# Reordering the attention steps of a hybrid encoder: first scores, two projection tiles and the transposes of V

## The reference

```
for l in range(2):
    h = rms_norm(x, attn_norm_g[l]);  parts = split(h @ w_in[l])
    ya = banded_attention(rope(qa), rope(ka), va, 128, sink)      # 8 query heads, 2 kv heads
    for window, dilation in ((128, 1), (512, 4), (2048, 16)):     # 4 heads each
        o, lse = dilated_attention(rope(qg), rope(kg), vg, window, dilation)
    yb = sum(softmax(lse) * o)                                     # over the three groups
    x = x + (sigmoid(gA) * (ya @ w_branch_a) + sigmoid(gB) * (yb @ w_branch_b)) @ w_out
    x = x + hier_moe(rms_norm(x, ffn_norm_g[l]))                   # 32 experts, two per token
return rms_norm(x, final_norm_g)
```

## Time and profile before

| | us |
|---|---|
| median of 3 runs (lowest, highest) | 1330.33 (1329.66, 1333.43) |
| span of the profiled execution | 1327.3 |
| PE busy | 1199.9 (90%) |
| DVE busy | 548.4 (41%) |
| ACT busy | 408.8 (31%) |
| POOL busy | 242.5 (18%) |
| idle of PE before its weight matmuls of the experts, waiting for their DMA | 38.4 |

### The profile page before, as it was taken

The page is one execution under the profiler, slowest core; times in us unless marked ns, Lnnn a source line. Parts: engine busy times, 40 slices in busy tenths (PEclk is TensorE's granted clock), DMA queues, the critical chain, the costliest instruction groups (busy, mean ns, idle before and its releaser), DMA issues.

```text
span 1327.3 us, 17358 instructions
## 1 busy us (share of the span) xinstructions
PE 1199.9 (90%) x6332; PEld 787.9 (59%) x6332; DVE 548.4 (41%) x1376; ACT 408.8 (31%) x822; POOL 242.5 (18%) x179
## 2 busy tenths in 40 slices
PE   7999998999988998889589999899999999988981
PEld 5777777888875443333177777778887844433320
DVE  4557664323344322222355676553333442322115
ACT  5344456333242111001244444563323411110002
POOL 0324510222201111111012353002221011111100
PEclk9999999999998999999899999999999999999996
DMA  5333311653746999999833333126437479999995
GB/s 199 114 98 101 96 57 34 206 189 100 255 171 213 404 425 422 425 422 412 320 96 103 96 96 96 33 87 218 156 110 286 166 273 410 423 423 424 420 412 232
DMA packets 69438, 305.97 MB, mean 231 GB/s; under 512 B 11968, under 2 KB 12224, under 8 KB 59120
## 3 DMA queue, kind: packets, MB, share of 16 engines
q1 hardware_dynamic: 58624, 282.45, 56.8%
q0 software_dynamic: 10592, 21.71, 4.4%
q10 hardware_dynamic: 144, 0.77, 0.2%
HBM read 289.68 MB, written 23.07 MB: 236 GB/s over the span
## 4 chain that ended last, share of the span: by engine, by line
PE 67%; DMA 16%; SPq 5%; DVE 5%; ACT 4%; issue 2%; DVEq 1%; POOLq 0%; ACTq 0%
PE bank L541 14%; PE bank L543 13%; PE bank L542 13%; DMA gu<-in_gu_w 12%; PE bank L840 10%; PE bank L856 4%; SPq L400 4%; DMA raw<-in_stream 2%; PE bank L650 2%; PE bank L679 2%; SPq L405 2%; PE bank L614 1%; PE bank L835 1%; PE bank L783 1%; DMA yld<-y_rows 1%
## 5 line engine op out<-in xcount | busy, mean ns | idle before, releaser
L840 PE MATMUL bank<-gu,xgt 128*64 128x512 f32 x1024 | 240.2, 619 | 40.1 <-DMA gu<-in_gu_w 38.4
L541 PE MATMUL bank<-h_hi,w_hi 128*128 128x512 f32 x640 | 253.1, 395 | 4.5 <-DVE h_lo L1280 3.5
L543 PE MATMUL bank<-h_hi,w_lo 128*128 128x512 f32 x640 | 249.4, 390 | 0.0
L542 PE MATMUL bank<-h_lo,w_hi 128*128 128x512 f32 x640 | 249.1, 389 | 0.0
L1235 DVE TENSOR_TENSOR w_lo<-raw,w_hi 128x1024 fp32r<-128x1024 f32 x102 | 131.2, 1287 | 176.9 <-ACT w_hi L968 176.9
L840 PEld LDWEIGHTS bank<-gu,xgt 128*64 128x64 f32 x1024 | 75.2, 142 | 201.1 <-issue 151.9
L541 PEld LDWEIGHTS bank<-h_hi,w_hi 128*128 128x128 f32 x640 | 120.2, 188 | 29.5 <-issue 3.4
L543 PEld LDWEIGHTS bank<-h_hi,w_lo 128*128 128x128 f32 x640 | 120.1, 188 | 25.4
L542 PEld LDWEIGHTS bank<-h_lo,w_hi 128*128 128x128 f32 x640 | 120.3, 188 | 23.8
L968 ACT ACTIVATE w_hi<-raw 128x1024 fp32r<-128x1024 f32 x102 | 107.4, 1053 | 59.7 <-PE bank L543 56.2
L856 PE MATMUL bank<-dn,zt 128*64 128x512 f32 x512 | 117.0, 599 | 6.3 <-ACT zt L1196 2.8
(11 more groups left out here) (186 smaller groups left out, 1596.3 us busy)
## 6 DMA issues: line engine op xcount, KB each, us to landing
gu<-in_gu_w SPq DMA_DIRECT2D x18, 4096.0 KB, 33.0
raw<-in_stream SPq DMA_DIRECT2D x112, 512.0 KB, 3.6
dn<-in_dn_w SPq DMA_DIRECT2D x18, 2048.0 KB, 35.6
gu<-in_gu_w SPq DMA_DIRECT2D x32, 1024.0 KB, 14.9
dn<-in_dn_w SPq DMA_DIRECT2D x20, 1024.0 KB, 18.9
gu<-in_gu_w SPq DMA_DIRECT2D x32, 512.0 KB, 5.4
swp<-pj SPq DMA_DIRECT2D x136, 64.0 KB, 2.3
dn<-in_dn_w SPq DMA_DIRECT2D x16, 512.0 KB, 5.8
```

The costliest lines, as they stand in the source:

```text
L541: mm(dst, ah, bh, start=start, stop=False)
L542: mm(dst, ah, bl, start=False, stop=False)
L543: return mm(dst, al, bh, start=False, stop=stop)
L840: last = mm(bank[b][e * CAP:(e + 1) * CAP, :], xgt[:, x_s, k, e * CAP:(e + 1) * CAP], gu[w_s][:, e, k, :], start=k == 0, stop=k == KD - 1)
```

## The change

It alters the list alone. Scores 0 moves from behind tile 6 to between tiles 4 and 5; scores 1 and 2 follow tile 5; tiles 6 and 7, which stood before transpose 0, go to steps 0 and 1, and all later tiles move with them, so that steps 0 to 16 and 18 hold a tile. Steps 12 and 15, which held none, now have tiles 18 and 21. Turn 21 stands behind tile 22 in step 16. In the two steps that hold no tile and have a turn (17 and 19) the turn stands behind values and scores. The number of instructions stays the same.

```diff
-FILLED = (*range(12), 13, 14, 16, 18)
+FILLED = (*range(17), 18)
@@ attention_order
-    for i in range(BLOCK_AT[1] + 1):
+    for i in range(BLOCK_AT[1]):
         order.append(("tile", i))
         if i == 1:
             order.append(("turn", 0))
-    order += [("scores", 0), ("scores", 1), ("scores", 2)]
-    waiting, nxt = [BLOCK_AT[1]], BLOCK_AT[1] + 1
-    order += [("turn", waiting.pop()), ("tile", nxt)]
-    if QKV[nxt][1] == V:
-        waiting.append(nxt)
-    nxt += 1
+        if i == BLOCK_AT[1] - 2:
+            order.append(("scores", 0))
+    order += [("scores", 1), ("scores", 2)]
+    waiting, nxt = [], BLOCK_AT[1]
@@
         if u in FILLED:
             next_tile()
-        elif waiting:
-            order.append(("turn", waiting.pop(0)))
@@
         if u + 3 < STEPS:
             order.append(("scores", u + 3))
+        if u not in FILLED and waiting:
+            order.append(("turn", waiting.pop(0)))
```

## The result

| | before | after |
|---|---|---|
| median of 20 runs each (lowest, highest), us | 1328.92 (1324.49, 1334.69) | 1332.98 (1326.71, 1339.55) |
| span of the profiled execution, us | 1327.3 | 1330.5 |
| PE busy, us | 1199.9 | 1208.4 |

The ratio is 1.0032 with an interval of 1.0018 to 1.0045: the change made the kernel slower by 0.3%, 4.1 us. The prediction was +1.4 us, "within 0.3%", with 1326.5 to 1338.0 as its range. The time is in the range, but the change costs 2.7 us more than forecast, and 1.0032 lies just beyond the 0.3% within which the likeliest case had it. That the median of 1332.98 came within 1.3 us of the 1331.7 forecast is in part luck: the forecast stood on the three runs before, whose median was 1.4 us above that of the twenty.

What follows compares the result with a forecast made beforehand. PE was taken to bound the stage, so its waits count, once in each layer. Layer 0: +0.5 - 2.7 - 0.3 + 2.7 = +0.2 us; layer 1 +1.2; together +1.4, giving 1331.7 us, range 1326.5 to 1338.0.

Steps and rivals of the forecast that it cites:

- the likeliest case: Whole kernel: +1.4 us, to 1331.7 us; alone 1329.5 to 1334; chance 0.48.
- Steps 12 and 15: Waits before transposes 13 and turn 21 go once these steps hold tiles: -2.7 us a layer.
- turn 22: Behind scores 20: a 1.1 us wait for copy_v(22) replaces its 1.4 us wait, -0.3 us a layer.
- The third rival: Waits of steps 12 and 15 return in the longer steps behind them; 1337.1 us, chance 0.07.
- The wait at transposes 20: PE waits 4.2 us at the h=1 half, as copy_v(23) comes after split_lo(24) and maxima(22) on DVE.
- The second rival: Wait of transposes 20 costs nothing at the stage's end; 1326.3 us, or 1325.9 with 2.2 at the start; chance 0.14.
- Turn 23: Behind scores 22, near the stage's end: late copy_v(23) and a lowered clock, +2.7 us a layer.
- The first term: Turn 23's late copy_v(23) delays transposes 20 and exps(22), so the stage ends 2.2 us later.
- gate 0 behind it has room before transposes 22 are wanted: Step 20, behind transposes 20: slow clock there delays ACT only through the four transposes left, 1.0 instead of 0.5 us.
- the +0.5 for the clock: Lowered clock behind the idle in transposes 20: +0.5 us a layer, ends 0 and 2.7.
- The start: Before transposes 0: a 2.4 us wait replaces the earlier waits, +0.5 us in layer 0 and +1.5 in layer 1.
- the first rival: POOL's add precedes `rca`; transposes 0 wait 3.6 us and the clock falls in tile 6; 1337.5 us, chance 0.24.

Runs made afterwards that it cites:

- the kernel with the waits filled: Changed kernel with unread matmuls put in the waits before transposes 0 and in transposes 20; 1329.82 us, ratio 1.0013 to the kernel before.
- both mended: Changed kernel with scores 1 ahead of tile 5, turn 23 directly behind transposes 19, split 24 a step earlier; 1319.53 us, ratio 0.9937 to before.
- tile 6 first: Changed kernel with tile 6 ahead of transposes 0, no tile in step 16, turn 23 back and split 24 earlier; 1327.57 us, ratio 0.9997 to before.

## Why the prediction fell short, step by step

**What held.** The direction, slower, and the terms of the middle and of the tail. Steps 12 and 15: forecast -2.7 us a layer, and turn 22 -0.3; the stretch of 158 to 206 us, which before holds steps 12 to 18 and not only to 16, as the prediction calls it, has 2.95 us less idle time. The third rival is out. The wait at transposes 18: 1.1 forecast, 1.2 measured. The wait at transposes 20: 4.2 forecast, 4.3 measured, by the chain that was named, ACT's split_hi(24), split_lo(24), maxima(22), copy_v(23). The kernel with split 24 moved shows that link: 1.4 us. The fall of the clock behind it came too. The second rival is out.

**Turn 23, +2.7 us forecast, +3.2 and +2.8 measured** (end of transposes 19 to transposes 23: 19.3 us before; after 22.54 in layer 0 and 22.10 in layer 1). The first term, 2.2 us, is 2.35 by the kernel with the waits filled, and 2.33 with the turns alone. In this term the step that failed is "gate 0 behind it has room before transposes 22 are wanted", and with it the +0.5 for the clock. I had counted only the four transposes that ACT waits for. PE's own path was slow for longer: from the second half of transposes 20 to gate 0 it takes 6.03 us (212.89 to 218.92) instead of 3.59 before (4.33 less the 0.74 of a wait). Those 2.4 us used up the slack that PE had at transposes 21 and 23, 0.7 and 1.6 us, and PE came onto the chain: ACT waited for PE at transposes 22, and transposes 23 wait 0.24 us where it was 1.58. The clock's term was 0.9 in layer 0 and 0.45 in layer 1, where 0.5 was forecast, and nothing with the turns alone: its size was about right on average, and the reason given for it was not.

**The start, +0.5 and +1.5 us forecast, about +2.6 and +2.2 measured** (up to the end of transposes 19 the layers changed by -0.38 and -0.81 us; take away the -3.0 of steps 12 to 18). That is most of the miss. These two are what is left over, not measured by themselves. Added up from their own rows they are +2.9 and +2.7 (waits of 3.2 against 1.9, and of 2.5 against 1.2 with one of 0.3 us on `w_lo` that the earlier trace rows left out; tile 6 1.6 and 1.4); the 0.3 and 0.5 us between weren't taken apart. Two steps failed. One is "if DVE goes on without letting POOL in, transposes 0 wait 2.4 us; if POOL is let in, 3.6. I take 2.4": in layer 0 POOL was let in, and the wait was 3.2, short of the 3.6; in layer 1 it was 2.5. The reason I gave, that DVE leaves no gap to POOL, doesn't hold: there is none between split_lo(6) and `rca`, and POOL went between. The other, dearer step is that I tied the clock in tile 6 to the wait being over 3.42 us, the longer idle of the earlier trace rows, and so put it into the first rival alone. It fell behind 3.2 us, behind 2.5 us, and in the kernel with `rca` from the bank behind 2.2 us. Tile 6 cost 1.6 us by that in layer 0 and 1.4 in layer 1 (transposes 0 and tile 6 take 7.67 and 7.46 us, and 6.06 where the wait was filled). The row at 1.42 us and the row at 3.42 us left it open for any idle between; the forecast's wait of 2.4 lay right there, and I should have carried half of that price in the likeliest case.

**The sum with these terms.** Layer 0: +2.6 - 3.0 + 3.2 = +2.8, measured +2.87. Layer 1: +2.2 - 3.0 + 2.8 = +2.0, measured +2.00. That it closes proves nothing, since the first term of each was taken from the total. Of the +4.9 us, the clock accounts for about 4 (2.4 and 1.7 in the kernel with the waits filled, 0.3 of it the shorter chain of DVE). The forecast's start was 2.8 us too low over both layers, and the result stayed in the range because the range had been made to take in the first rival, of which a part came true.

**What stays open.** Why layer 1 meets POOL differently from layer 0 in one execution and not in the next (waits before transposes 0 of 3.2 and 2.5 us after, 3.1 and 3.8 with turn 23 back) wasn't tested. By the timelines it hangs on where POOL stands when split_lo(6) ends, and so on when the four swap DMAs land. What makes the clock fall behind a wait of 1.9 us in one execution and not in the next is open too. The 1.7 us that lie outside the stages were not tested either.

## What to carry to other kernels

When a reordering trades many short waits for fewer long ones, compare the lengths and not only the sums: each wait long enough to lower the matrix engine's clock costs its own length and then up to 2.7 us of slow work behind it, and matmuls that nobody reads, put into the wait, take that second price back. Before an entry is put later in a list that several engines walk, look on each of them at what it is now queued behind; here a copy of 0.7 us made PE wait 4.3, of which 2.3 to 3.2 came through at the end, and 2.9 of the wait went when the unrelated weight split ahead of it was moved. Read busy time beside idle time: the same matmuls with more busy time is the first sign of the clock. Two mends of one chain need not add: each took the tail to less than 19.4 us, and both together no further than the better one (18.75).

## What the runs showed of the hardware

**Who goes next between two DVE instructions.** DVE and POOL exclude each other when DVE's operands both lie in SBUF, and where POOL was waiting as such a DVE instruction ended, POOL went next, although DVE had its next one ready: `rca` took 1.63 us here and 1.75 with turn 23 back, with 0.69 when undisturbed. One operand from the accumulator bank instead takes DVE out of it: 0.69 us in the middle of POOL's add. The Trainium skill, "SBUF — State Buffer", section "SBUF: two separate sides", describes an exclusive lock held for a whole instruction. The traces agree with it, and with its reading that the prediction had set aside, POOL asked first and went first.

**Which idles lowered the clock.** In this stage it fell behind each of PE's waits of 2.2, 2.5, 3.1, 3.2, 3.7, 3.8 and 4.3 us, and behind none of 1.2 to 1.6 us. Waits of 1.9 us before transposes 23 lie between: of the eight in four kernels (split 24 earlier, waits filled, both mended, tile 6 first) it fell behind two and stayed up behind six. Nor does the length alone decide: ahead of layer 1's stage, in the transposes of the norm, PE of the kernel before idles 2.58 us, and the 32 behind it take 3.86 us at a granted clock of 1.00:

```profile
666.78 3.86 PE L570 MATMUL bank<-cst,xn 128*128 128x128 f32 x32 [2.58 <-DVE xn L1259]
```

The cost behind it was not fixed: after the change tile 6 was slow for its first ten matmuls or so (1.6 us), and with split 24 earlier it lost 2.7 us (8.72 instead of 6.06).
